# A hybrid transformer layer with expert gathers: the order in branch B, the first query, the modulation loads and the split of seven weight loads

## The reference

```
mod = (silu(c) @ w_mod + b_mod).reshape(bsz, 6, 1, d)          # shift, scale, gate, twice
n = rms_norm(h, norm1_g) * (1.0 + scale1) + shift1
ya, yb, yc = sparse_attention(n), stick_breaking(n), gated_linear(n)
gates = sigmoid(n @ w_gl + b_gate)                             # three of them
y = (gates[0] * (ya @ w_oa) + gates[1] * (yb @ w_ob) + gates[2] * (yc @ w_oc)) @ w_out
h = h + gate1 * y
n = rms_norm(h, norm2_g) * (1.0 + scale2) + shift2
# expert retrieval: 8 heads, 16 of 16384 experts for each head and token
q = (n @ w_pq).reshape(T, 8, 2, 128)
s = einsum('nhpd,hpkd->nhpk', q, sub_keys)                     # 128 keys twice
top_s, top_i = top_k(s, 16);  best_s, best_j = top_k(all pair sums, 16)
g = softmax(best_s);  expert = the pair's index
act = gelu(einsum('nd,nhkd->nhk', n, u_tab[expert]))
h = h + gate2 * einsum('nhk,nhkd->nd', g * act, v_tab[expert])
```

## Time and profile before

| | |
|---|---|
| median of three runs | 2069.91 us (2068.1 to 2070.54) |
| profiled execution, its time | 2072.25 us |
| span of the profiled execution | 2070.1 us |
| mean granted TensorE clock | 0.911 |
| busy: PE, DVE, POOL, ACT | 1680.6, 1455.1, 633.8, 578.4 us |
| gathers' queue | 73728 packets, 536.90 MB, 62.9% of the time of 16 DMA engines |
| all transfers | 658.72 MB, mean 318 GB/s |

### The profile page before, as it was taken

How to read it: one execution, slowest core, us unless ns; L and a number is a source line. 1 busy time by engine, 2 the same in 40 slices (tenths; PEclk the granted TensorE clock), 3 DMA queues, 4 the chain that set the end, 5 groups by cost and what they waited for, 6 DMA issues and landing times.

```text
span 2070.1 us, 17694 instructions
## 1 busy us (share of the span) xinstructions
PE 1680.6 (81%) x5546; PEld 933.8 (45%) x5546; DVE 1455.1 (70%) x3352; ACT 578.4 (28%) x1263; POOL 633.8 (31%) x542
## 2 busy tenths in 40 slices
PE   4999999899897999998888766777887766667665
PEld 3443445667787565565555323333443222222222
DVE  5346551668316787887787998887777878887876
ACT  2111122666213443542222223222222222222221
POOL 0000000120001334333434454544444444444441
PEclk8999899999998999999999888888898888888889
DMA  9442120011337999999999999999999999999995
GB/s 369 183 180 89 56 100 41 31 52 71 135 112 293 390 419 416 416 412 419 402 411 400 419 420 384 419 420 420 419 419 421 420 419 420 420 420 419 420 419 230
DMA packets 89502, 658.72 MB, mean 318 GB/s; under 512 B 9776, under 2 KB 10944, under 8 KB 16192
## 3 DMA queue, kind: packets, MB, share of 16 engines
q0 software_dynamic: 73728, 536.90, 62.9%
q1 hardware_dynamic: 14032, 119.18, 14.5%
q10 hardware_dynamic: 1648, 1.51, 0.2%
HBM read 653.95 MB, written 3.34 MB: 318 GB/s over the span
## 4 chain that ended last, share of the span: by engine, by line
PE 40%; DMA 36%; DVE 10%; issue 7%; ACT 4%; POOL 2%; SPq 0%; DVEq 0%; POOLq 0%; ACTq 0%
DMA sb<-uv_table,sb 34%; PE ps L1066 10%; PE ps L641 6%; PE ps L643 4%; PE ps L960 3%; PE ps L748 3%; DVE sb L1949 3%; DVE sb L1973 2%; PE ps L762 2%; POOL sb L2097 2%; PE ps L988 2%; PE ps L924 1%; PE ps L993 1%; DMA sb<-w_mod 1%; PE ps L579 1%
## 5 line engine op out<-in xcount | busy, mean ns | idle before, releaser
L1066 PE MATMUL ps<-sb 128*128 128x512 f32 x1424 | 776.8, 691 | 289.2 <-ACT sb L1442 284.5
L2097 POOL DMA_INDIRECT sb<-uv_table,sb x512 | 606.8, 1185 | 883.9 <-PE ps L1066 664.7
L1949 DVE CUSTOM_DVE_ANT_0 sb<-sb 128x1024 f32<-128x1024 f32 x512 | 625.6, 1222 | 244.5 <-DMA sb<-uv_table,sb 235.6
L1066 PEld LDWEIGHTS ps<-sb 128*128 128x128 f32 x1424 | 290.3, 215 | 724.9 <-ACT sb L1442 419.4
L1442 ACT ACTIVATE sb<-sb 128x128 f32<-128x128 f32 x356 | 132.7, 399 | 610.2 <-DVE sb L1958 605.0
L1973 DVE SCALAR_TENSOR_TENSOR sb<-sb 128x512 f32<-128x512 f32 x304 | 214.7, 748 | 2.2
L1431 ACT ACTIVATE sb<-sb 128x2 f32<-128x2 f32 x256 | 52.1, 204 | 398.7 <-DVE sb L1949 398.2
L2066 POOL TENSOR_TENSOR sb<-sb 128x128 f32<-128x128 f32 x8 | 13.1, 1638 | 444.1 <-DVE sb L1691 444.1
L641 PE MATMUL ps<-sb 128*128 128x512 f32 x304 | 138.5, 608 | 0.0
L960 PE MATMUL ps<-sb 128*128 128x256 f32 (+1 forms) x608 | 125.1, 362 | 5.6 <-DMA sb<-w_pq 5.3
L960 PEld LDWEIGHTS ps<-sb 128*128 128x128 f32 x608 | 106.4, 202 | 34.3 <-issue 16.6
(11 more groups left out here) (264 smaller groups left out, 1774.1 us busy)
## 6 DMA issues: line engine op xcount, KB each, us to landing
sb<-w_mod SPq DMA_DIRECT2D x12, 2048.0 KB, 12.5
sb<-w_pq SPq DMA_DIRECT2D x18, 1152.0 KB
sb<-w_merge SPq DMA_DIRECT2D x24, 768.0 KB
sb<-w_proj SPq DMA_DIRECT2D x8, 2048.0 KB, 8.5
sb<-w_merge SPq DMA_DIRECT2D x6, 2304.0 KB, 8.8
sb<-uv_table,sb POOLq DMA_INDIRECT x512, 27.6
sb<-w_merge SPq DMA_DIRECT2D x3, 1536.0 KB, 6.6
sb<-w_out SPq DMA_DIRECT2D x4, 1024.0 KB, 11.9
```

Source lines behind the costliest of these rows:

```text
L1066: mm = pe.matmul(bank(2 * (t % 2) + f), dgw[m % NDG], row_v(n)[:, T * f:T * (f + 1)], start=(i == 0), stop=(i == PH * PK - 2))
L1949: dve.tensor_tensor_reduce(out=row_u(n), in0=row_u(n), in1=n2_tm(u // PH), scale=1.0, scalar=0.0, op0=ALU.mult, op1=ALU.add, accum_out=dot ...
L2097: pool.indirect_dma_start(out=ring[PLACE[n]], out_offset=None, in_=uv_table, in_offset=bass.IndirectOffsetOnAxis(ap=experts[u % 4][:, i:i ...
```

## The change

It has five parts.

- **Modulation loads.** `vec` is loaded up to column `V_ONG` = 102 first; its other 512 columns come after the small constants, and PE's square sums and POOL's `rgain` wait for them. The last 2 MB tile of the first third of `w_mod` is loaded as two halves with a semaphore each.
- **Branch B.** On PE `out_product` is that of head `it−1` and stands right behind z, and `gate_product(it)` stands behind `lt`. On ACT the gate's tanh stands behind beta's exp. On DVE `merge(it−1)` stands behind min.
- **First query.** `first_query()` stands behind `output(1, 3)`, not `output(1, 5)`, and runs over the eight operands with both halves of the result in turn; `score(0)` stands behind `output(1, 4)`.
- **Merges of the second half.** Slot 0 has none any more and slot 29 has one: merges 1 to 17 stand one place of the list later.
- **Weights of the last seven loads of queries** come in two transfers, partitions 0 to 119 and 120 to 127.

```
@@ sync @@
-            sp.dma_start(area("vec", 0, V_END), vec).then_inc(ld_vec, 16)
+            sp.dma_start(area("vec", 0, V_ONG), vec[:, 0:V_ONG]).then_inc(ld_vec, 16)
...
-                sp.dma_start(dst, src).then_inc(w_in[place], 16)
+                if (kind, i) == ("mod1", 3):
+                    sp.dma_start(dst[:, 0, :], src[:, 0, :]).then_inc(w_in[place], 16)
+                    sp.dma_start(dst[:, 1, :], src[:, 1, :]).then_inc(s["mod1_last"], 16)
+                else:
+                    sp.dma_start(dst, src).then_inc(w_in[place], 16)
...
                     sp.dma_start(walpha, w_alpha).then_inc(ld_small, 16)
+                    sp.dma_start(area("vec", V_ONG, T), vec[:, V_ONG:V_END]).then_inc(ld_small, 16)
...
                 if LOADED[q] > LOADED[q - 1]:
                     sp.wait_ge(s["sc_done"], q)
-                    sp.dma_start(pq_slot, w_pq[QUERIES[q][0]]).then_inc(s["ld_pq"], 16)
+                    rows = (0, 120, P) if QUERIES[q][1] >= H else (0, P)
+                    for lo, hi in zip(rows, rows[1:]):
+                        sp.dma_start(pq_slot[lo:hi], w_pq[QUERIES[q][0]][lo:hi]).then_inc(s["ld_pq"], 16)
@@ PE, branch B @@
-                    gate_product(it)
                 if 1 <= it <= HB:
+                    out_product(it - 1)
                     h = it - 1
                     pe.wait_ge(s["keep_ready"], h + 1)
...
                 if it < HB:
-                    out_product(it)
+                    gate_product(it)
@@ PE, first query @@
+            def first_query():
+
+                pe.wait_ge(s["ld_pq"], 16)
+                w = pq_slot[:, 0:2 * D].rearrange("p (i k n) -> p i k n", i=2, k=KT)
+                for k in range(KT):
+                    pe.wait_ge(s["n2_ready"], k + 1)
+                    for c in range(2):
+                        mm = pe.matmul(bank(6, P, H * c), w[:, c, k, :], n_t[:, k, 0:P], start=(k == 0 and c == 0),
+                                       stop=(k == KT - 1), skip_group_check=True)
+                mm.then_inc(s["q_done"], 1)
...
-                elif (t, c) == (1, 5):
-                    query(0, 0)
-                    query(0, 1)
-                elif (t, c) == (1, 6):
+                elif (t, c) == (1, 3):
+                    first_query()
+                elif (t, c) == (1, 4):
                     score(0)
@@ merges @@
-            [0, 3, 4, 7, 8, 11, 12, 15, 16, 19, 20, 22, 23, 24, 26, 27, 28, 30, 31, 32, 33, 34, 35])}
+            [3, 4, 7, 8, 11, 12, 15, 16, 19, 20, 22, 23, 24, 26, 27, 28, 29, 30, 31, 32, 33, 34, 35])}
...
-            merge_products(MERGE_SLOT[0])
@@ ACT, branch B @@
-                    gate(it)
...
                     act.activation(beta[h % 3], beta[h % 3], ACT.Exp).then_inc(s["a_exp"], 1)
+                if it < HB:
+                    gate(it)
@@ DVE @@
+                if k == KT - 1:
+                    dve.wait_ge(s["mod1_last"], 16)
...
+                if it >= 1:
+                    merge(it - 1)
...
-                if it < HB:
-                    merge(it)
```

More of the change, by code:

```diff
@@ L377, in encoder_layer @@
         v_step = sem("v_step")
-        names = """csig cact_ready mod1_sum mod1_used mod2_used xss_ready xvar_ready xrt_ready xr_ready xhat_ready mod_done
+        names = """csig cact_ready mod1_sum mod1_last mod1_used mod2_used xss_ready xvar_ready xrt_ready xr_ready xhat_ready mod_done
                    mod_read tr_done nt_ready proj_done proj_out sq_ready sq_used stat_var stat_rt
@@ L446, in encoder_layer @@
         NQ, EARLY_Q = len(QUERIES), 3
-        LOADED = [sum(r == 0 or QUERIES[r][0] != QUERIES[r - 1][0] for r in range(q + 1)) for q in range(NQ)]
+        LOADED = [sum((r == 0 or QUERIES[r][0] != QUERIES[r - 1][0]) * (1 + (QUERIES[r][1] >= H)) for r in range(q + 1))
+                  for q in range(NQ)]
         QUERY_SLOT = {4 * (q - 3) + 1: q for q in range(3, 11)}
@@ L597, in _ @@
             turn(KT - 1)
-            pe.wait_ge(ld_small, 3 * 16)
+            pe.wait_ge(ld_small, 4 * 16)
             def square_sums(i):
@@ L950, in query @@
                     pe.wait_ge(s["ld_pq"], LOADED[q] * 16)
-                    if q >= 1:
-                        pe.wait_ge(s["n2_ready"], KT * min((lo + n) // P, 3))
+                    pe.wait_ge(s["n2_ready"], KT * min((lo + n) // P, 3))
                     pe.wait_ge(s["q_out"], q)
@@ L957, in query @@
                 for k in range(KT):
-                    if q == 0 and c == 0:
-                        pe.wait_ge(s["n2_ready"], k + 1)
                     mm = pe.matmul(bank(6 if q < EARLY_Q else 4, n, H * c), w[:, c, k, :], n_t[:, k, lo:lo + n],
@@ L1130, in _ @@
                             score(q)
-                if slot in MERGE_SLOT and slot > 0:
+                if slot in MERGE_SLOT:
                     merge_products(MERGE_SLOT[slot])
@@ L2075, in _ @@
             pool.wait_ge(s["rsil"], 1)
+            pool.wait_ge(ld_small, 4 * 16)
             pool.tensor_tensor(rc, rc, vcol(V_ONG, T).unsqueeze(1).broadcast_to([P, TT, T]), ALU.mult).then_inc(s["rgain"], 1)
```

## The result

The changed kernel takes 2103.7 us (median of four runs, 2100.03 to 2105.13) against 2069.01 of before in the same runs: ratio 1.0171, interval 1.0154 to 1.0188. It is 34.7 us slower where 12.4 us less were forecast. Its profiled span is 2097.9 us.

What follows compares the result with a forecast made beforehand. Compute chains bound it before 640 us, DMA bytes from the first gathers on, one late DMA engine about 11 us of the end. −0.8 + 1.3 − 1.3 − 2.6 + 1.0 − 10.0 = −12.4, from 2069.9 to 2057.5 us; 8-in-10 range 2053.5 to 2070.5.

Steps and rivals of the forecast that it cites:

- Modulation loads: Start of the kernel: less transfer ahead of w_mod and an earlier start on its last tile, −0.8 us.
- Branch B: Reordered loop before the gathers: start −2.85, loop +0.6, tail +3.6, sum +1.3 us, bounds −1 and +3.6.
- First query: Ahead of the gathers: first pick about 4 us earlier, taken as −1.3 us, bounds 0 and −2.8.
- Merges: Second half: DMA hole at 690 to 710 us closes, −2.6 us; ten merges in a row cost +1.0.
- Weights in 120 and 8 partitions: Last seven query loads: same bytes, other engines carry them; −10.0 us, late-engine bounds −19.7 and +2.5.
- The second half of the step: End of the kernel: the late DMA engine is the one left out by 120 partitions, taken as −10.0 us.
- Start: Branch B's first iteration: z(1) no longer behind out_product(0), −2.85 us.
- Loop: Branch B's iterations: the gate's tanh behind exp beta adds 0.1 us each, +0.6 over six.
- Tail: Branch B's end: tanh(7), out_product(7) and lt(7) delay the last yb's start by 3.6 us.
- the ring: Gather buffers: full, so PE sets when POOL goes on; POOL's ninth gather waited 16.82 us for PE's weighing.
- The ten merges in a row: Rival, second half: PE's waits for half merges empty the ring; slower, placed at 2076 us, chance 0.07.
- that the split moves nothing: Rival, last seven loads: even spread or late engine keeps its 8 rows; 2067.5 us, chance 0.19.

Runs made afterwards that it cites:

- no split: The changed kernel with its seven late loads in one transfer of 128 partitions again: 2068.28 us, ratio 1.0007 to the kernel before.
- 64 and 64: The changed kernel with its seven late loads cut into 64 and 64 partitions: 2097.03 us, ratio 1.0164 to the kernel before.
- a load alone: The changed kernel with the late loads whole and only the first query-weight load, at 552 us without gathers, in 120 and 8 partitions: 2064.03 us, one run.
- the three parts: Modulation loads, first query and merges together, without the split and with branch B as before: ratio 0.9989 to the kernel before, again 0.9986 (2064.85 us).

## Why the prediction was wrong, step by step

**Weights in 120 and 8 partitions.** This step failed. It said that the bytes are the same, and that what changes is who carries them. The bytes are the same and the time to carry them is not: a row of such a load takes about 600 ns in place of 352, and each gather's row beside it 540 to 580 in place of 313. The second load lasts 11.3 us in place of 5.5; over seven that is 7 x 5.8 = 41 us, and the split alone measured +39 (36 to 47 by its interval). The bounds, −19.7 and +2.5, came only from rows that count rows per engine; nothing bounded a row's price, since the trace of before has no load of another shape in this stage. The nearest rows in it would have misled: two copies of 64 partitions of 2048 B from on-chip memory to on-chip memory, issued by ACT at 84.19 and 128.51 us, have median packets of 84 ns (the slowest 204), as rows of 2048 B in its loads of 128 partitions have; they are small, four rows for each engine. The bound that was missing is a doubling: when a shape is new to the trace, its price per packet is as open as its share.

The second half of the step failed too. The late engine is not the one left out. The end marks of two gathers, the 227th and the last, stand as follows, in us after the first mark (one for each of the 16 engines, in order of time):

```
changed   1306.9  0.0 2.5 2.7 2.7 2.7 2.7 2.8 2.8 2.8 3.0 3.2 3.2 3.2 3.4 3.5 3.9
          2067.9  0.0 2.0 3.9 3.9 4.0 4.5 4.5 4.7 5.1 5.2 5.8 6.4 6.6 6.9 8.2 18.8
no split  1309.8  0.0 0.2 0.2 0.2 0.4 0.4 0.5 0.6 0.6 0.6 0.7 0.7 1.0 1.0 1.0 1.4
          2041.2  0.0 0.2 0.2 0.7 0.8 1.8 2.0 2.0 2.2 2.3 2.5 2.6 2.6 3.7 4.1 13.9
```

After the first split load one engine is 2.5 us ahead of all others, about the 2.8 us that 8 rows were reckoned at, and 5.1 and 7.6 us after the second and the third; with 64 and 64, where all 16 take part, none is (0.1 us). Its lead never falls under 2.0 us up to the end, so it is another engine that is last there, 18.8 us behind, as one is without the split. That lag also grows where none of these loads is under way: without the split from 6.1 us at 1601 to 13.9 at 1999. So the relief would have gone to the wrong engine even at the old price. Of the rules weighed, the choice of 15 engines by the Trainium skill ("DMA: Bandwidth & Descriptors", "Why a DMA increments its semaphore by 16 and not by 1") agrees with the 15 + 8 end marks seen for each load. The rule of "Rules for kernel authors" to use one 128-partition transfer holds here, though not for the reason given there: two transfers by columns cost nothing. A section that I had not weighed, "The descriptor swizzle", says that in a 128-partition transfer each engine writes one port of the on-chip memory, four rows here and four there. That other shapes lose this is an inference which fits (a load alone at half rate, reading unharmed, 64 as bad as 120); no run here shows a port.

**Branch B.** The sign was right, the size was not: +1.3 forecast, +4.3 measured (2.1 to 6.6). Inside the stage the profile with branch B alone gives it term by term. Start: Abs(1) follows Abs(0) 2.6 us sooner (22.07 in place of 24.62; −2.85 forecast). Loop: Abs(1) to Abs(7) takes 91.83 us in place of 90.54, +1.3 where +0.6 was forecast (+0.4 in the changed kernel). Tail: forecast +3.6, it took 25.14 in place of 19.67, +5.5 (+5.4 in the changed kernel), and in the latter 1.5 of the 1.8 us over the forecast are the slower clock behind PE's new wait, which I had not priced. Together that is +4.2 up to the last yb. But at the first pick only 1.2 of it are left (633.82 − 336.05 = 297.77 in place of 296.58), partly because the four outputs before it ran at a granted clock of 1.00 there and 0.83 before (7.31 us in place of 8.94). So how +4.3 reach the end is open.

**First query.** Alone it brings the first pick 5.1 us forward, counted from branch B's first Abs (626.35 − 334.84 = 291.51 in place of 296.58), and 3.5 and 4.5 us in the two profiles of the three parts, around the 4 us forecast. A part of the gain and its spread is PE's clock: my 2.2 us for an output came from a stretch at 0.83, and two outputs take 3.74 us in one of these profiles and 5.37 in another. In the time no gain shows: forecast −1.3, measured within −0.8 and +4.1. The hole behind it stays open: the share of 690 to 710 us is still 0.87. Yet from the first gather's packet to the last it takes 1410.5 us in this profile and in that of before, so between these two single executions the earlier start did reach the end. What it is worth is open; that the ring sets the pace there is not tested.

**Merges.** Right: −2.6 + 1.0 = −1.6 forecast, −2.9 measured (−0.4 to −5.2), and the hole closed. The ten merges in a row, my slower rival, cost nothing that shows: PE's wait for the half merges is 12.0 us in 8 waits in the changed kernel (12.1 in 9 with the merges alone), before 11.5 in 6. The row of the changed kernel, where the second merge product is L1009 (us in total, times, longest us):

```profile
PE ps L1009 <- DVE sb L1853: 12.0, 8, 2.6
```

**Modulation loads.** −0.8 forecast, and not resolved: no run has this part alone. PE's first projection starts at 43.52 us in the changed kernel and 43.69 before, but over the profiles it is 43.45 to 43.80 without this part and 43.19 to 43.70 with it.

None of the rivals was the one that came. The nearest, that the split moves nothing, had the split at no price, where it cost 39 us. One sum of the prediction is off by a little: the lower bounds named for its range add up to 2053.2 us, not 2053.5.

## What to carry to other kernels

Load into all 128 partitions, and cut by columns when a transfer has to be cut: in these loads a row cost 1.5 to 2 times as much with 112, 120 or 64 partitions. This is shown for pieces of 64 partitions and more with rows of 9216 B from device memory; what the pieces of 8 partitions cost by themselves is not. Read GB/s beside the DMA share, because an engine that is slowed is as busy as one at full rate. And when an order puts a wait in front of PE as long as the 3.27 us here, price what runs behind it at the lower clock.

## What the runs showed that I had not expected

The second load, in pieces of 120, 112 or 64 partitions, takes 531 to 699 ns (medians) for a row of 9216 B that takes 347 to 354 ns in a load of 128, and the gathers' rows beside it take 476 to 602 ns in place of 313; a copy of 120 rows from device memory to device memory keeps 326 ns. PE's clock fell to 0.58 over 4 us after an idle stretch of 3.27 us, and a product of 2.00 us took 3.50.
